# Rotary exchange of halves: two ScalarE copies across partitions in place of a permutation product on TensorE

## What is computed

```python
def _rope(x, pos):
    half = x.shape[-1] // 2
    inv = ROPE_BASE ** (-jnp.arange(half, dtype=jnp.float32) / half)
    ang = pos.astype(jnp.float32)[:, None] * inv[None, :]
    cos = jnp.cos(ang)[None, :, None, :]
    sin = jnp.sin(ang)[None, :, None, :]
    x1, x2 = x[..., :half], x[..., half:]
    return jnp.concatenate([x1 * cos - x2 * sin, x1 * sin + x2 * cos], axis=-1)

# in each layer, B_HEADS = 4 heads of B_HD = 128
qb = _rope(_heads(qb, B_HEADS), pos)
kb = _rope(_heads(kb, B_HEADS), pos) * (B_HD ** -0.5)
ob, ret_new = _retention(qb, kb, _heads(vb, B_HEADS), ret.astype(f32), log_gamma)
```

## Time and profile before

| what | value |
|---|---|
| time, median of 3 runs | 2808.72 us (2807.89 to 2815.1) |
| time of the profiled execution | 2807.61 us |
| its span, first to last instruction | 2805.9 us |
| mean granted TensorE clock | 0.975 of full |
| PE busy | 2636.4 us (94%) |
| DVE busy | 1134.1 us (40%) |
| ACT busy | 684.6 us (24%) |
| POOL busy | 1378.5 us (49%) |

### The profile page before, as it was taken

One profiled execution on the slowest core, in us unless ns is written; L12 is line 12 of the kernel. 1 busy time (PEld: TensorE's weight loads), 2 busy tenths in 40 slices (PEclk: granted clock), 3 DMA queues, 4 the chain that ended last, 5 costly groups with the idle time before them and its releaser, 6 DMA issues.

```text
span 2805.9 us, 66257 instructions
## 1 busy us (share of the span) xinstructions
PE 2636.4 (94%) x25812; PEld 2496.3 (89%) x25812; DVE 1134.1 (40%) x1758; ACT 684.6 (24%) x1196; POOL 1378.5 (49%) x1179
## 2 busy tenths in 40 slices
PE   5999999999999899999989999999999998999997
PEld 5889889898899899999978898988988898999996
DVE  4535535345246421114445353452453554111244
ACT  3323213223133111112232132231332322110122
POOL 4435346154246545556653461552543564555564
PEclk9999999999999999999989999999999999999998
DMA  5112122022136322212321221221212452222122
GB/s 175 58 52 96 46 74 94 26 89 71 36 100 213 105 68 90 90 53 82 107 83 46 75 85 35 85 76 36 101 55 67 138 163 82 86 90 90 53 79 82
DMA packets 84542, 233.61 MB, mean 83 GB/s; under 512 B 12176, under 2 KB 16288, under 8 KB 83312
## 3 DMA queue, kind: packets, MB, share of 16 engines
q1 hardware_dynamic: 66672, 188.40, 20.7%
q10 hardware_dynamic: 14112, 29.63, 2.8%
q0 software_dynamic: 3552, 12.56, 1.3%
HBM read 198.57 MB, written 31.98 MB: 82 GB/s over the span
## 4 chain that ended last, share of the span: by engine, by line
PE 76%; DVE 11%; PEld 4%; issue 3%; ACT 2%; DMA 1%; POOL 1%; SPq 0%; DVEq 0%; ACTq 0%; PEldq 0%; POOLq 0%
PE psP L639 41%; PE psQ L639 14%; PE psQ L703 10%; PEld psP L639 3%; PE psQ L696 3%; PE psQ L978 2%; PEld psQ L639 1%; PE psQ L951 1%; PE psP L968 1%; PE psP L703 1%; DMA W<-in_w_br 1%; DVE BIG L1555 1%; DVE BIG L1504 1%; PE psQ L943 1%; PE psP L962 1%
## 5 line engine op out<-in xcount | busy, mean ns | idle before, releaser
L639 PE MATMUL psP<-HH,WS 128*128 128x272 f32 x4256 | 871.4, 302 | 54.1 <-DVE BIGR L1478 19.9
L497 POOL TENSOR_SCALAR WS<-W 128x512 fp32r<-128x512 f32 (+1 forms) x392 | 294.2, 751 | 901.7 <-PEq L633 496.8
L639 PEld LDWEIGHTS psP<-HH,WS 128*128 128x128 f32 x4256 | 654.4, 192 | 90.4 <-issue 45.6
L639 PE MATMUL psP<-HH,WR 128*128 128x272 f32 x2240 | 471.9, 293 | 0.0
L639 PE MATMUL psP<-HL,WS 128*128 128x272 f32 x2240 | 471.5, 292 | 0.0
L499 POOL TENSOR_TENSOR WR<-W,WS 128x512 fp32r<-128x512 f32 x280 | 391.0, 1396 | 23.4
L639 PEld LDWEIGHTS psP<-HL,WS 128*128 128x128 f32 x2240 | 360.5, 193 | 0.0
L639 PEld LDWEIGHTS psP<-HH,WR 128*128 128x128 f32 x2240 | 359.8, 194 | 0.0
L703 PE MATMUL psQ<-BIG 64*64 64x64 f32 (+1 forms) x5696 | 275.5, 232 | 42.2 <-DVE BIG L1661 15.9
L639 PE MATMUL psQ<-HH,BIGR 128*128 128x272 f32 x1760 | 305.5, 287 | 0.0
L703 PEld LDWEIGHTS psQ<-BIG 64*64 64x64 f32 x5696 | 220.6, 134 | 89.4 <-issue 72.8
(11 more groups left out here) (270 smaller groups left out, 3301.8 us busy)
## 6 DMA issues: line engine op xcount, KB each, us to landing
W<-in_w_stage SPq DMA_DIRECT2D x88, 512.0 KB, 3.7
W<-in_w_f SPq DMA_DIRECT2D x88, 512.0 KB, 3.6
W<-in_w_gate SPq DMA_DIRECT2D x48, 512.0 KB, 3.8
W<-in_w_f SPq DMA_DIRECT2D x88, 256.0 KB, 2.6
gates_waiting<-GB ACTq DMA_DIRECT2D x48, 272.0 KB, 4.2
BIG<-gates_waiting SPq DMA_DIRECT2D x48, 272.0 KB, 3.0
W<-in_w_br SPq DMA_DIRECT2D x48, 256.0 KB, 2.7
W<-in_w_out SPq DMA_DIRECT2D x16, 512.0 KB, 3.6
```

Of the source, the lines that this page charges most:

```text
L497: pool.tensor_scalar(high, src, 1.0, 0.0, ALU.mult, ALU.add).then_inc(high_part[q], 1)
L639: mm = pe.matmul(out[:, a, 0:HT], a_, x_[:, a * HT:(a + 1) * HT], start=(first and n == 0), stop=(last and n == 2))
```

## The change

The permutation product goes. Instead ScalarE copies the lower half of the tile to the upper half of the scratch tile `T[4]` and the upper half to the lower (`halves_swapped`), for the query between the copy of C0 and the I2 copies, for the key between the M1 copies and the copy of C1. The sign moves into the sine table. VectorE multiplies `T[4]` by the sine and the tile by the cosine, each in place (`turned`), and adds them (`rotated`): for the query the two products stand before the I4 additions and the sum behind them, for the key before and behind the M4 additions. One constant, its transfer and two uses of the PSUM turns are gone; a semaphore `B_rot` is new. The key's copies wait until the query is rotated, because both use `T[4]`.

```diff
--- before.py
+++ after.py
@@ -85,7 +85,7 @@
 GR = range(GROUPS)
 SMALL_A = ([f"score{g}" for g in GR] + ["B_vt"] + [f"{n}{g}" for n in ("tok", "L") for g in GR]
            + [f"I1{g}" for g in GR] + ["bonus"] + [f"{n}{g}" for n in ("I2", "I3", "I4", "M1") for g in GR]
-           + ["B_ropeq"] + [f"{n}{g}" for n in ("M2", "M3") for g in GR] + ["B_ropek"] + [f"{n}{g}" for n in ("M4", "WQ") for g in GR]
+           + [f"{n}{g}" for n in ("M2", "M3", "M4", "WQ") for g in GR]
            + [f"{n}{c}" for c in range(8) for n in ("U", "S")] + ["XT", "U8", "C_vt", "S8", "A_mean"])
 B_AND_C = ["B_sc", "B_kt", "A_var", "C_sc0", "B_kv", "C_sc1", "B_dkv", "C_sc2", "C_sc3", "C_sc4", "B_mean", "C_sc5",
            "B_var", "C_sc6", "C_sc7", "C_kt", "C_kv", "C_dkv", "C_var"]
@@ -169,7 +169,7 @@
 PRODUCTS = """par shift_diff shout xm0 xm1 xm2 pads xv_pads kkr sq floor ln rn kk kt k2 beta bsum dc dca ea er ek pc
  ar_a ar_r bt ktl bonus n16 l lo t1 nl4 l8
  sdec um vm A_sq A_rstd A_n A_y2 A_o
- B_g B_c0 B_c1 B_q B_k B_qd B_vm B_s B_sq B_rstd B_n B_o
+ B_g B_c0 B_c1 B_rot B_q B_k B_qd B_vm B_s B_sq B_rstd B_n B_o
  C_g C_f0 C_f C_k0 C_qp C_tot C_vm C_s C_dk C_sq C_rstd C_n C_o C_lvl C_add""".split()
 
 
@@ -839,12 +839,6 @@
                                 heads(b[:, 0, 128 * i:128 * i + 64], off[:, c], TT[cur][:, c])
                                 mm = heads(b[:, 0, 128 * i + 64:128 * i + 128], TT[cur][:, c], K["eye64"])
                             filled(f"M{step}{g}", mm)
-                        if step == 1:
-                            wait_emptied(pe, l, ph, turn, "B0")
-                            square(l, ph, turn, "B_ropeq", K["swap"][:], UB[:, 0:TOK])
-                        else:
-                            wait_emptied(pe, l, ph, turn, "B1")
-                            square(l, ph, turn, "B_ropek", K["swap"][:], UB[:, TOK:2 * TOK])
                         fill(f1, f2)
                         for g in GR:
                             after(f"M{step}{g}")
@@ -1249,6 +1243,15 @@
                         b = wait_full(act, l, ph, turn, f"I1{g}")
                         taken(f"I1{g}", NL2[:, c:c + PER], b[:, 0, 0:384].rearrange("p (a b d) -> p a b d", b=2, d=HD))
                     evacuate("C", 0)
+                    def halves_swapped(n):
+
+                        u = (BQ, BK)[n]
+                        wait_emptied(act, l, ph, turn, f"B{n}")
+                        act.activation(T[4][0:HD], u[HD:P], ACT.Copy)
+                        act.activation(T[4][HD:P], u[0:HD], ACT.Copy).then_inc(S[f"B_c{n}"], 1)
+
+                    act.wait_ge(S["ar_r"], it1)
+                    halves_swapped(0)
                     for g in GR:
                         c = PER * g
                         b = wait_full(act, l, ph, turn, f"I2{g}")
@@ -1269,6 +1272,8 @@
                             m = prompt_chunks(g)
                             taken(f"M{step}{g}", ZD[:, c:c + m], b[:, 0, 0:128 * m].rearrange("p (a b d) -> p a b d", b=2, d=HD))
                         if step == 1:
+                            act.wait_ge(S["B_q"], it1)
+                            halves_swapped(1)
                             evacuate("C", 1)
                     for g in GR:
                         c = PER * g
@@ -1619,23 +1624,19 @@
                         b = filled("B2")
                         emptied_by("B2", tt(halves(UB[:, 2 * TOK:3 * TOK]), halves(UB[:, 2 * TOK:3 * TOK]), pair(b), ALU.mult))
 
-                    def cosine(n):
-
+                    def turned(n):
+
+                        u = (BQ, BK)[n]
+                        w(S[f"B_c{n}"])
+                        tt(T[4], T[4], K["sin"][:], ALU.mult).then_inc(S["B_rot"], 1)
                         after(f"B{n}")
-                        tt(T[5], (BQ, BK)[n], K["cos"][:], ALU.mult).then_inc(S[f"B_c{n}"], 1)
-
-                    def sine(n):
-
-                        u, use = (BQ, BK)[n], ("B_ropeq", "B_ropek")[n]
-                        b = filled(use)
-                        w(S[f"B_c{n}"])
-                        emptied_by(use, tt(halves(u), halves(K["sin"][:]), pair(b), ALU.mult))
+                        tt(u, u, K["cos"][:], ALU.mult).then_inc(S["B_rot"], 1)
 
                     def rotated(n):
 
                         u = (BQ, BK)[n]
-                        after(("B_ropeq", "B_ropek")[n])
-                        tt(u, u, T[5], ALU.add).then_inc(S[("B_q", "B_k")[n]], 1)
+                        dve.wait_ge(S["B_rot"], it * 4 + 2 * n + 2)
+                        tt(u, u, T[4], ALU.add).then_inc(S[("B_q", "B_k")[n]], 1)
                         w(S[("B_q", "B_k")[n]])
 
                     gate_of_b()
@@ -1672,11 +1673,10 @@
                     bonus()
                     for use, bank, src, other in (("I2", 1, 0, "nl4"), ("I3", 1, 1, "l8"), ("I4", 1, 0, None),
                                                   ("M2", 0, 1, None), ("M4", 0, 0, None)):
-                        if use == "M2":
-                            cosine(0)
-                            sine(0)
+                        if use == "I4":
+                            turned(0)
                         elif use == "M4":
-                            sine(1)
+                            turned(1)
                         for g in GR:
                             c = PER * g
                             b = filled(f"{use}{g}")
@@ -1685,10 +1685,10 @@
                             m = PER if use == "I2" else prompt_chunks(g)
                             emptied_by(f"{use}{g}", tt(TT[1 - src][:, c:c + m], TT[src][:, c:c + m],
                                                        blocks(b[:, bank, 0:HD * m], HD), ALU.add))
-                        if use == "M2":
+                        if use == "I4":
                             rotated(0)
-                            cosine(1)
-                    rotated(1)
+                        elif use == "M4":
+                            rotated(1)
                     dve.wait_ge(sd_in["A"], it * 16 + 16)
                     w(S["pc"])
                     tt(blocks(SD[:, 0:512], HD), blocks(SD[:, 0:512], HD), bc(PC[:, 8:16], 2, HD), ALU.mult).then_inc(S["sdec"], 1)
@@ -1903,7 +1903,7 @@
 
 RC_M, RC_MD, RC_QD, RC_KD, RC_G, RC_W = 0, 128, 160, 292, 294, 296
 CONST_SHAPES = {
-    "eye128": (P,), "eye64": (HD,), "heads1": (P,), "headsmean": (P,), "mean128": (P,), "swap": (P,),
+    "eye128": (P,), "eye64": (HD,), "heads1": (P,), "headsmean": (P,), "mean128": (P,),
     "eps": (3,), "lnhalf": (1,), "cos": (TOK,), "sin": (TOK,), "reset": (TOK,), "mnr": (2, 128), "ml": (2, HD),
     "m16": (HD,), "m32": (HD,), "m64": (HD,), "maskb": (DEC_B,), "maskd": (DEC_B,), "hm": (8, C), "hmd": (3, DEC),
     "rc": (STAGES, RC_W),
@@ -1926,16 +1926,12 @@
     k = {"eye128": np.eye(P, dtype=f), "eye64": np.tile(np.eye(HD, dtype=f), (2, 1))}
     same = (i[:, None] // HD == i[None] // HD).astype(f)
     k["heads1"], k["headsmean"], k["mean128"] = same, same / HD, np.full((P, P), 1 / P, f)
-    swap = np.zeros((P, P), f)
-    swap[i[HD:], i[HD:] - HD] = -1
-    swap[i[:HD], i[:HD] + HD] = 1
-    k["swap"] = swap
     k["eps"] = np.tile(np.array([1e-6, 64e-5, 1e-5], f), (P, 1))
     k["lnhalf"] = np.full((P, 1), 0.5 * math.log(LN_SCALE), f)
     pos = np.where(t < SEQ, t, 4096 + (t - SEQ) % DEC_T).astype(f)
     inv = (f(10000.0) ** (-np.arange(HD, dtype=f) / f(HD))).astype(f)
     ang = (inv[:, None] * pos[None]).astype(f).astype(np.float64)
-    k["cos"], k["sin"] = (np.tile(g(ang), (2, 1)).astype(f) for g in (np.cos, np.sin))
+    k["cos"], k["sin"] = (np.concatenate((s * g(ang), g(ang))).astype(f) for g, s in ((np.cos, 1), (np.sin, -1)))
     start = np.where(t < SEQ, t % HD == 0, (t - SEQ) % DEC_T == 0)
     k["reset"] = np.tile((~start).astype(f), (P, 1))
     s, u = i[:HD, None], i[None, :HD]
```

## The result

The changed kernel takes 2775.5 us (median of four runs, 2773.1 to 2784.8) against 2808.3 us: a ratio of 0.989, 95% interval 0.9872 to 0.9908. The gain is 33 us by these medians and 28.5 us by the means of all runs of both kernels whose span and clock are on record (85 of before, 10 of after: 2807.4 and 2778.9 us).

The account below looks back on a forecast made before the run. TensorE's instruction stream, busy 94% of the span, was taken to set the pace. -14.6 + 0.8 = -13.8 us on 2807.6 gave 2793.8; with the median 1.1 us above the profiled execution, the forecast was 2795 us, range 2789 to 2804.

Parts of the forecast that it names:

- The squares: TensorE, behind M1 and M3: two permutation products per stage leave, 16 x 0.91 = 14.6 us saved, 13.0 by the lower figure.
- the 0.8 us between gross and net: VectorE ahead of I4: 0.1 us per stage allowed for semaphores between the query's two products, 0.8 us lost in all.
- Rival (d): TensorE: the squares fill a hole in which it would otherwise wait, so nothing changes, 2808 us; chance 0.03.
- The ScalarE copies: ScalarE: four crossing 64x544 copies per stage at 0.66 us; the query's pair, 1.32 us, hides in 1.50 us idle before I2.
- Rival (b): ScalarE late at I2: a crossing copy takes 2.3 us, so the kernel is slower, +11.0 us, 2819.7; chance 0.07.
- The key's pair: ScalarE before the copy of C1: two copies, 1.32 us, fit in 1.33 us idle; priced at nothing.
- The VectorE products: VectorE between the I3 and I4 additions: the query's two products, 1.44 us undisturbed, fit in 1.54 us idle.
- rival (a): VectorE late at I4: both products run at 1.35 us, 9.3 us lost, net -5.3 us, 2803.4; chance 0.10.
- GpSimd's scaling copy: GpSimd in the gap before I4, 0.35 us per stage beside VectorE's products: taken to cost about nothing.
- the upper bound: VectorE's two products ahead of I4 at 2 x 1.68 = 3.36 us: 1.82 us lost per stage, 14.6 us.
- the protection that the sine product gave up: VectorE: the old PSUM operand avoided contention with GpSimd; with two SBUF operands the loss is at most 14.6 us.
- The clock: TensorE's granted clock: 1.2 us lost per drop, three drops more or fewer 3.7 us either way, no sign.

Follow-up runs that it names:

- `again`: The changed kernel once more, unedited, in turns with the kernel before: mean 2780.0 us, ratio 0.9902 to before, 105.6 us at half clock.
- `four_columns_in_place`: Changed kernel plus one unread four-column product behind M1 and one behind M3: mean 2797.5 us, ratio 0.9967 to before, 130.0 us at half clock.
- `dummies_in_place`: Changed kernel with two unread squares of the old size per stage put back behind M1 and M3: mean 2809.3 us, ratio 1.001 to before.
- `four_elsewhere`: Changed kernel plus four old-size squares per stage behind the sixth and seventh level of branch C: mean 2814.1 us, ratio 1.0026 to before.
- `four_columns_moved`: Changed kernel with one four-column product behind I4 and one behind M2, not behind M1 and M3: mean 2792.0 us, ratio 0.9944 to before.
- `squares_at_bonus`: Changed kernel plus two old-size squares per stage ahead of the bonus square, which stands ahead of I2: mean 2807.7 us, ratio 1.0006 to before.

## Why the prediction was wrong

**The squares: right.** The step priced a square at 0.91 us from the earlier trace rows. In the changed timeline a stage is 1.84 us shorter for two of them, and products of the same size put in elsewhere cost 0.86 to 0.90 us each. Forecast -14.6 us gross and -13.8 net; measured -13.6 at full clock. That the two agree to 0.2 us is partly luck: the 0.8 us between gross and net wasn't lost where it was put (below), the measured figure is uncertain by more than 1 us, and at 0.41 us per us of half-clock time it would be 16. Rival (d), a hole behind the squares, is out: none appeared.

**The ScalarE copies: right.** A crossing copy takes what the nearest row took, 0.66 us, and the pair fits into the gap of 1.50 us with 0.15 us to spare (forecast 0.18). Rival (b) is out: all 32 take 655 to 660 ns, by the line view of the changed kernel (count, then shortest, median and longest ns). The key's pair was rightly priced at nothing: no wait of TensorE for it appears.

```profile
L1250 ACT ACTIVATE BIG<-UB x16: 655/657/660, 130.4 to 2084.7; 64x544 f32<-64x544 f32 x16
L1251 ACT ACTIVATE BIG<-UB x16: 656/657/657, 131.1 to 2085.4; 64x544 f32<-64x544 f32 x16
```

**The VectorE products: right, the allowance too high.** The two ahead of I4 take 0.72 us each and overlap in the record, so they need 1.36 us of the 1.54. The I4 addition waits for TensorE, not TensorE for it, so the 0.8 us allowed for semaphores isn't lost, and rival (a) is out. The prediction let GpSimd's scaling copy run beside these products and took it to cost nothing. That wasn't put to the test: the products now stand so early in the gap that GpSimd is busy for only 0.61 us beside them in all eight stages. One reading was off: of the 1.68 us of the cosine at 149.17 only 1.10 us lay beside the subtraction, which ended at 150.27; the upper bound and the price of (a) rest on that row, the forecast doesn't. The key's products are disturbed as the rows of GpSimd's subtraction let one expect:

```profile
148.75 1.00 DVE L1631 TENSOR_TENSOR BIG<-BIG,c_sin 128x544 f32<-128x544 f32 x1
149.68 1.79 DVE L1633 TENSOR_TENSOR UB<-UB,c_cos 128x544 f32<-128x544 f32 x1
153.16 0.71 DVE L1686 TENSOR_TENSOR BIG<-BIG,psQ 128x192 f32<-128x192 f32 x2 [1.69 <-PE psQ L703]
```

They take 1.00 and 1.79 us here, much the same in all eight stages, and VectorE still waits 1.69 us for TensorE before M4. So the protection that the sine product gave up was lost only where it is covered.

**The clock: the step that failed.** The prediction said "three drops more or fewer are 3.7 us either way. I have no reason for a sign." Measured: 30 us less half-clock time, some 12 to 15 us of gain, about as much as the work that was taken away. The term was mis-sized at the root. It took one place of one stage pair for the size of the effect, 1.2 us lost per drop, and three drops for its spread. But the mean clock of 0.975 in the table of the kernel before already says 140 us at the lower level, some 70 us lost, and single runs of one kernel differ by 7 to 16 us (standard deviation) in it. An edit that shifts TensorE's stream in each of eight stages can move a part of those 70 us, and 3.7 us was no bound for that. In hindsight, a range widened by 15 us either way would have held the result.

The Trainium skill, "TensorE: Matmul & The Clock Gate", Part 1 (the HAM clock gate), puts the cost of the ramp, the slow products at a kernel's start, below 1% of a typical kernel's span and advises against fitting to a count of them. It also says that this count varies from run to run of one kernel. The half-clock time of this kernel varies so too (7 to 16 us), but it isn't such a ramp: it is spread over the run, 133 us are 4.8% of the span and cost about 2.4%, and the difference between the two kernels is 0.5%.

**What stays open.** Shown: the additional gain is no scatter (`again`), doesn't come from ScalarE's or VectorE's order (`four_columns_in_place`, `dummies_in_place`), is not explained by the amount of work, which adds 13 us for four squares (`four_elsewhere`), doesn't hang on the neighbours of M1 and M3 (`four_columns_moved`, `squares_at_bonus`) nor on the distance from I1 to XT alone (the two kernels with moved steps). It comes from TensorE's stream: the squares put back bring all of it back. That it hangs on how the sparse places of that stream lie in time fits all of these, but is not shown: the moved steps also brought new waits. By what rule a given place falls to the lower clock was not found, and no kernel here predicts it. Summed over the profiled executions in windows of 1 us, the changed kernel's lower half-clock time (119 against 139 us) isn't in one place either: 7 us of the 20 lie within the eight stages, over several places, and 13 outside them, in parts that the change doesn't touch. These are single executions, and of the size of the scatter.

## What to carry to other kernels

Split each run's time by its span and granted clock before an edit is judged: the time at full clock gave the price of most edits here to 1 to 3 us where the medians were 15 us off. Where the mean clock is below 1, price the half-clock time as an account of its own, with its own spread, and take the range of a forecast from that spread when an edit moves TensorE's stream. A wait that every stage repeats can be worth nearly its full length at full clock (12.0 of 13.5 us here) once work is put ahead of the very group that waits; one group later it was worth nothing.

## What the runs showed of the hardware

A product of four columns, 0.25 us from its start to the next, put behind M1 and behind M3 in each stage brought 27 us more at 1.2 GHz over the run (103.3 to 130.0). Moving two filling steps, with no work added and TensorE busy 94% in all four kernels, brought 18 us in the kernel before and 57 us in the changed one, together with a new wait of 0.8 us per stage. Within the stages the profiles show the lower clock again and again behind the same places, the wait at I1 and the sixteen products of 128x4 in B's and in C's output, but each time in a part of the stages only. In the windows behind B's output TensorE shows as busy throughout at either level, so its busy time doesn't tell which one it had; only the granted clock and the count of records do. A ScalarE copy of 64x544 from one half of the partitions to the other took 655 to 660 ns, as long as one within a half (656).
